# First half of the first key and value projection computed between the two halves of the modulation

## What is computed

```python
mod_lat = silu(c) @ w_mod[l] + b_mod[l]          # [3*1024]; the same for c_ctx
shift, scale, gate = split(mod, 3)
h = rms_norm(x, norm_g) * (1 + scale) + shift    # latent and context rows, each with its own modulation
p = h @ w_in                                     # [512, 11424], split into columns:
qc, kvc, kr, dq, dk, dv, sq, sk, sv, z, gm = split_cols(p)
# kvc and kr: the compressed keys and values (256 columns) and the rotary key (32 columns)
```

## Time and profile before

| | |
|---|---|
| median of three runs | 2431.78 us |
| the profiled execution's own time | 2431.57 us |
| its span, from first to last instruction | 2429.8 us |
| PE busy | 2398.9 us, 99% |
| DVE busy | 1459.4 us, 60% |
| ACT busy | 1192.1 us, 49% |
| DMA in the first of 40 slices (60.7 us) | 7 tenths busy, 258 GB/s |

### The profile page before, as it was taken

One profiled execution on the slowest core, in us unless ns is written; L12 is line 12 of the kernel. 1 busy time (PEld: TensorE's weight loads), 2 busy tenths in 40 slices (PEclk: granted clock), 3 DMA queues, 4 the chain that ended last, 5 costly groups with the idle time before them and its releaser, 6 DMA issues.

```text
span 2429.8 us, 33585 instructions
## 1 busy us (share of the span) xinstructions
PE 2398.9 (99%) x12793; PEld 2013.3 (83%) x12793; DVE 1459.4 (60%) x2470; ACT 1192.1 (49%) x2278; POOL 100.0 (4%) x151
## 2 busy tenths in 40 slices
PE   8999999999999999899999999999999999999999
PEld 6978888788888888888887888888888888888887
DVE  4555564775667435565538676665679844566565
ACT  5553223743247332564337455564566555545643
POOL 1100000510000000000004000000000000000000
PEclk9999999999999999999999999999999999999999
DMA  7403543134430222234531523555555561655653
GB/s 258 109 23 113 165 148 87 45 119 133 147 87 10 91 84 80 80 105 139 144 90 61 178 84 100 198 172 186 178 177 178 190 189 52 208 176 161 201 170 131
DMA packets 165007, 318.80 MB, mean 131 GB/s; under 512 B 10470, under 2 KB 22624, under 8 KB 164336
## 3 DMA queue, kind: packets, MB, share of 16 engines
q1 hardware_dynamic: 161552, 303.67, 40.3%
q0 software_dynamic: 3296, 12.98, 1.9%
HBM read 313.46 MB, written 3.15 MB: 130 GB/s over the span
## 4 chain that ended last, share of the span: by engine, by line
PE 93%; DVE 3%; ACT 2%; issue 1%; DMA 1%; SPq 0%; POOL 0%; DVEq 0%; ACTq 0%
PE bank L895 25%; PE bank L897 24%; PE bank L896 24%; PE bank L937 7%; PE bank L1086 6%; PE bank L1048 1%; PE bank L1059 1%; PE bank L1065 1%; PE bank L1062 1%; PE bank L1213 1%; PE bank L1147 1%; DMA w_raw_more<-in_w_mod_dram 1%; DVE w_low_part L1807 0%; PE bank L1173 0%; PE bank L971 0%
## 5 line engine op out<-in xcount | busy, mean ns | idle before, releaser
L1807 DVE TENSOR_TENSOR w_low_part<-w_raw,w_high_part 128x1024 fp32r<-128x1024 f32 (+3 forms) x544 | 638.3, 1186 | 529.7 <-ACT w_high_part L1289 525.4
L1289 ACT ACTIVATE w_high_part<-w_raw 128x1024 fp32r<-128x1024 f32 (+3 forms) x544 | 553.9, 1031 | 711.0 <-PE bank L897 708.9
L895 PE MATMUL bank<-w_high_part,h_high 128*128 128x512 f32 (+3 forms) x2128 | 816.6, 384 | 3.6 <-DVE h_low L1845 1.7
L897 PE MATMUL bank<-w_high_part,h_low 128*128 128x512 f32 (+3 forms) x2128 | 806.8, 379 | 0.0
L896 PE MATMUL bank<-w_low_part,h_high 128*128 128x512 f32 (+3 forms) x2128 | 805.9, 379 | 0.0
L895 PEld LDWEIGHTS bank<-w_high_part,h_high 128*128 128x128 f32 x2128 | 400.1, 188 | 79.7 <-issue 3.9
L897 PEld LDWEIGHTS bank<-w_high_part,h_low 128*128 128x128 f32 x2128 | 399.9, 188 | 75.1
L896 PEld LDWEIGHTS bank<-w_low_part,h_high 128*128 128x128 f32 x2128 | 400.4, 188 | 71.1 <-issue 0.2
L1620 ACT ACTIVATE stage<-bank,neg_max 128x512 f32<-128x512 f32 (+1 forms) x240 | 147.6, 617 | 112.6 <-DVE neg_max L2290 59.6
L1086 PE MATMUL bank<-v,probs_turned 128*128 128x128 f32 x1280 | 173.3, 275 | 0.0
L937 PEld LDWEIGHTS bank<-ident,stage 128*128 128x128 f32 (+1 forms) x1112 | 127.1, 139 | 52.3 <-issue 35.6
(11 more groups left out here) (318 smaller groups left out, 2550.0 us busy)
## 6 DMA issues: line engine op xcount, KB each, us to landing
w_raw<-in_w_in_dram SPq DMA_DIRECT2D x160, 512.0 KB, 3.6
w_raw<-in_a_w_in_dram SPq DMA_DIRECT2D x96, 512.0 KB, 4.1
w_raw<-in_b_w_in_dram SPq DMA_DIRECT2D x80, 512.0 KB, 4.6
w_raw<-in_w_branch_dram SPq DMA_DIRECT2D x48, 512.0 KB, 4.0
w_raw<-in_w_mod_dram SPq DMA_DIRECT2D x37, 512.0 KB, 4.0
w_raw<-in_a_w_out_dram SPq DMA_DIRECT2D x32, 512.0 KB, 4.2
w_raw<-in_c_w_in_dram SPq DMA_DIRECT2D x32, 512.0 KB, 4.1
w_raw<-in_w_out_dram SPq DMA_DIRECT2D x16, 512.0 KB, 3.9
```

Source lines behind the costliest of these rows:

```text
L895: pe.matmul(o, high, wh, start=(k == 0), stop=False)
L897: mm = pe.matmul(o, low, wh, start=False, stop=(k == u.kt - 1))
L1289: nc.scalar.activation(WH[:, n % PART_SLOTS, 0:kt, 0:width], raw[:, 0:kt, 0:width], ACT.Copy).then_inc(*S.up("w_high", c))
L1807: v.tensor_tensor(WL[:, s, 0:kt, 0:width], raw[:, 0:kt, 0:width], WH[:, s, 0:kt, 0:width].bitcast(F32), ALU.subtract).then_inc(*S.up("w_lo ...
```

## The change

Two of the four chunks of the first `kvc` projection are computed ahead of the last quarter of the work on the modulation. In the new order the list is: mod 0, mod 2, split of h0 and h1, split of h2 and h3, a new step `begin`, the rest of mod 1, mod 3, split of h4 to h7, and `kvc` with its chunks 2 and 3.

- On PE, `begin` is: `kvc` chunk 0 (24 matmuls), rides of the first three chunks of mod 1, `kvc` chunk 1 (24 matmuls). Then come the ride of the fourth chunk of mod 1 and mod 3 as before.
- The transposes h2 and h3 stand right behind `select` of mod 2, in the banks "out" (6 and 7). `select` of mod 1 and of mod 3 also use the banks "out".
- ACT and DVE prepare `kvc` chunk 0 at the head of the split of h0 and h1, chunk 1 behind the split of h3, chunk 2 behind h5, chunk 3 behind h7.
- The transfers go in the new order: mod 0, mod 2, `kvc` chunks 0 and 1, mod 1, mod 3, `kvc` chunks 2 and 3. The landing places follow: mod 1 lands in the places 7, 11, 8 and 12, which mod 2 had, so each of its transfers waits until the ride of mod 2 from that place is done.

```diff
-FIRST_LANDING = (7, 11, 8, 12, 5, 9, 6, 10, 0, 1, 2, 3, 4, 8, 12, 11, 0, 1, 2, 3, 4)
+FIRST_LANDING = (5, 9, 6, 10, 7, 11, 8, 12, 0, 1, 7, 11, 8, 12, 2, 3, 4, 0, 1, 2, 3)
...
+    def place_first(u, count):
+        u.pfirst = len(to_split)
+        u.opened = count
+        for chunk in u.chunks[:count]:
+            u.at.append(len(chunks))
+            to_split.append(len(chunks))
+            chunks.append(chunk)
+        steps.append(("begin", u))
...
             steps.append(("split_h", (0, 1)))
+            steps.append(("split_h", (2, 3)))
+            kvc = Unit("mla_c", ("kvc", l), ALL_TILES, ("h", l), w_in, D, OFF_KV, KVR + ROT, off=QR)
+            place_first(kvc, 2)
             place(modulation_unit(0, 1))
-            steps.append(("split_h", (2, 3)))
             place(modulation_unit(0, 3))
...  PE
+            def begin(u):
+                sums = [other for other in units if other.key == ("mod", 0, 1)][0]
+                chunks_of(u, None, 0, 1)
+                for n in range(3):
+                    ride(sums, n, "out")
+                chunks_of(u, None, 1, 2)
+
             def gemm(u, turned):
                 if u.kind == "mod":
                     j = u.key[2]
-                    for n in range(len(u.chunks)):
+                    for n in range(3 if j == 1 else 0, len(u.chunks)):
                         if (j, n) == (2, 1):
                             select(0, 0, "wide")
                         if (j, n) == (3, 2):
-                            select(0, 1, "wide")
-                        for k in {(2, 2): (0,), (2, 3): (1,), (1, 3): (2,), (3, 0): (3,)}.get((j, n), ()):
+                            select(0, 1, "out")
+                        for k in {(2, 2): (0,), (2, 3): (1,)}.get((j, n), ()):
                             turn(*h_piece(0, k, "turn"))
                         ride(u, n, "out" if j % 2 else "wide")
...
                 elif j > 1:
-                    select(l, j, "wide")
-                    if j == 3:
-                        for k in (6, 7):
-                            turn(*h_piece(0, k, "out"))
+                    select(l, j, "wide" if j == 2 else "out")
+                    for k in (2, 3) if j == 2 else (6, 7):
+                        turn(*h_piece(0, k, "out"))
...  ACT (DVE alike)
-                    if u.key[2] == 3:
-                        prepare(1)
                     take_modulation(u.key)
-                    if u.key[2] == 3:
-                        prepare(2)
...
+            def begin(u):
+                prepare(2)
+
             def split_h(which):
+                if which[0] == 0:
+                    prepare(1)
...
-                    if k > 4:
-                        prepare(k - 3)
+                    if k in (5, 7):
+                        prepare(3 if k == 5 else 4)
```

More of the change, by code:

```diff
@@ L153, in __init__ @@
         self.pfirst = self.plast = None
+        self.opened = 0
 def plan():
@@ L167, in plan @@
     riding = [(sums, m) for sums in (modulation_unit(*lj) for lj in SUMMED) for m in range(D // (P * KT))]
+    def place_first(u, count):
[6 more added lines that the diff above has]
+        steps.append(("begin", u))
     def place(u):
-        u.pfirst = len(to_split)
-        for n, chunk in enumerate(u.chunks):
+        if not u.opened:
+            u.pfirst = len(to_split)
+        for n, chunk in list(enumerate(u.chunks))[u.opened:]:
             u.at.append(len(chunks))
@@ L214, in plan @@
             steps.append(("turn_h", l, 1))
-        gemm("mla_c", ("kvc", l), ALL_TILES, ("h", l), w_in, D, OFF_KV, KVR + ROT, off=QR)
+        if l == 0:
+            place(kvc)
+        else:
+            gemm("mla_c", ("kvc", l), ALL_TILES, ("h", l), w_in, D, OFF_KV, KVR + ROT, off=QR)
         steps.append(("mla_norm", l, "kv", ALL_TILES))
@@ L849, in turn_late @@
                     late.append((n, piece))
+            def begin(u):
[4 more added lines that the diff above has]
+                chunks_of(u, None, 1, 2)
             def gemm(u, turned):
-                open_banks = {}
                 if u.kind == "mod":
                     j = u.key[2]
-                    for n in range(len(u.chunks)):
+                    for n in range(3 if j == 1 else 0, len(u.chunks)):
                         if (j, n) == (2, 1):
@@ L858, in gemm, with chunks_of @@
                         if (j, n) == (3, 2):
-                            select(0, 1, "wide")
-                        for k in {(2, 2): (0,), (2, 3): (1,), (1, 3): (2,), (3, 0): (3,)}.get((j, n), ()):
+                            select(0, 1, "out")
+                        for k in {(2, 2): (0,), (2, 3): (1,)}.get((j, n), ()):
                             turn(*h_piece(0, k, "turn"))
                         ride(u, n, "out" if j % 2 else "wide")
-                    if j == 3:
-                        for k in (4, 5):
-                            turn(*h_piece(0, k, "turn"))
+                    for k in (4, 5) if j == 3 else ():
+                        turn(*h_piece(0, k, "turn"))
                     return
-                for n, (src, k0, kt, col, width) in enumerate(u.chunks):
+                chunks_of(u, turned, u.opened, len(u.chunks))
+                if turned and not turns_inside(u):
+                    turn_qk(turned)
+            opened = {}
+            def chunks_of(u, turned, start, stop):
+                open_banks = opened.setdefault(u.key, {})
+                for n, (src, k0, kt, col, width) in list(enumerate(u.chunks))[start:stop]:
                     while late and late[0][0] <= n:
@@ L903, in gemm @@
                             mm.then_inc(*S.up("w_used", c))
-                if turned and not turns_inside(u):
-                    turn_qk(turned)
             def ride(u, n, pool="out"):
@@ L1246, in store @@
                 pass
-            todo = dict(gemm=gemm, vectors=vectors, condition=condition, modulation=modulation, norm=norm, small=small,
+            todo = dict(gemm=gemm, begin=begin, vectors=vectors, condition=condition, modulation=modulation, norm=norm, small=small,
                         turn_h=turn_h, split_h=split_h, turn_h2=turn_h2, mla_norm=mla_norm, turn_c=turn_c,
@@ L2068, in modulation @@
                 key = ("turn", "mod", l, j)
-                if (l, j) == (0, 3):
-                    prepare(1)
                 dve.wait_ge(*S.filled(key))
@@ L2174, in split_h @@
                                     ALU.subtract).then_inc(*S.up("spare_read", key))
-                    if k > 3:
-                        prepare(max(2, k - 3))
+                    if k in (5, 7):
+                        prepare(3 if k == 5 else 4)
                 spares[0] += len(which)
```

## The result

| | before | changed |
|---|---|---|
| median of 12 runs each | 2431.91 us | 2437.14 us |
| lowest to highest | 2431.21 to 2434.23 | 2435.84 to 2441.99 |
| profiled execution, its span | 2429.8 us | 2435.2 us |
| T, ACT's first h4 | 36.46 | 42.68 |
| start of `qc` | 50.13 | 55.55 |

The changed kernel is slower: ratio 1.0023, 95% interval 1.0015 to 1.0031, 5.2 us. The last row says where: everything behind the start of `qc` takes the same time, so the whole difference is made in the first 56 us.

A forecast was written before the change was run, and what follows sets the result against it. Before, transfers bound the modulation until 34 us; changed, PE's own queue would end it and the split stand uncovered. T 43.7 plus 12.2 puts `qc` at 55.9 against 50.13, +5.8 us: 2437.4 us, range 2434.3 to 2440.3.

The forecast's parts named there:

- T: ACT's first h4, after the modulation: forecast to move from 36.46 to 43.7 us.
- the forecast's own range: Total time of the changed kernel, central case: 2436.6 to 2438.8 us around 2437.4, given 55%.
- S: Start of kvc chunk 1 on PE: forecast 34.5 us, bounds 33.4 and 35.9.
- First fall of the clock: PE at kvc chunk 0: clock low from 28.0 to 31.4 us, 0.26 us a matmul, chunk ending at 32.85.
- T to qc: From ACT's first h4 to the start of `qc`: 12.2 us with a clock fall at chunk 2, bounds 12.0 and 13.7.
- The transfers don't set it: End of the modulation: last transfer lands near 34.8 us, but PE asks for it only at 40.7.
- Preparation of chunk 0 and the banks cost nothing: ACT and DVE prepare chunk 0 within existing waits, charged nothing; copies from banks 6 and 7 are over in time.
- Order on PE: PE's queue: matmuls stay in program order, so no ride can overtake kvc chunk 0 or 1.
- (a): Rival: inserted 6.3 us hide in PE's transfer waits, `qc` at 50.0, kernel not slower at 2431.5 us; 12%.
- (b): Rival: the clock doesn't fall, or falls once, giving 2436.0 to 2436.8 us; 22%.
- (c): Rival: the clock stays low through all of chunk 0 and chunk 2, giving 2439 to 2440.3 us; 11%.

The follow-up runs named there:

- e4: The kernel before, with SP issuing the first kvc transfer only after the ride of the first chunk of mod 3: 2431.90 us, ratio to before 0.9996 to 1.0014.
- e11: The kernel before plus the same single unused matmuls behind most rides as e10, as a control: 2431.51 us.
- e3: The changed kernel plus unused matmuls in two PE waits, 7 ahead of kvc chunk 0 and 10 ahead of chunk 2: 2438.94 us.
- e6: As e3, with two more unused matmuls behind each ride of mod 0 and mod 2, to hold the clock: 2436.31 us.
- e7: As e2, only kvc chunk 0 early, with the unused matmuls of e6 but none ahead of chunk 2: 2432.35 us.
- e1: The changed kernel with no kvc chunk early on PE, all four behind h7; transfers and preparation as changed: 2432.61 us.
- e2: The changed kernel with only kvc chunk 0 ahead of the rides on PE, chunk 1 behind h7 again: 2433.83 us.
- e9: The kernel before without its warm-up matmuls: 2432.03 us, ratio to before 0.9992 to 1.0010.
- e5: PE's order as in the kernel before, only transfers and preparation of kvc chunks 0 and 1 early as changed: 2432.26 us.
- e10: As e5, with one unused matmul behind most rides: 2432.36 us.
- e8: The changed kernel without the 26 warm-up matmuls of PE at the start: 2440.08 us.
- e12: Against the kernel before, only kvc chunk 0 sent ahead of mod 1, its four row tiles computed one by one between rides: 2435.44 us.

## Why the prediction was right

The time was 2437.14 for 2437.4 forecast, inside the forecast's own range, and slower.

- **T.** Forecast 43.7, measured 42.68. The step from S to T was 9.2 and is 9.11 (33.57 to 42.68). S was 0.9 early, since chunk 0 began at 27.15 instead of 28.0. That goes back to the last ride of mod 2, at 21.46 instead of 22.40 in the trace of before, which seems to have been a late one: e4, with the same transfers up to there, has it at 21.44, but e11 at 22.76.
- **First fall of the clock.** Forecast low from chunk 0's start to 31.4, measured from 28.0 to 31.4. The price was right, the path in part luck: chunk 0's first 0.8 us ran at 1.00, and the clock came back 4.3 us after its start, where I had 3.4. A matmul at 1.2 GHz took 0.24 us, where I had 0.26. Chunk 0 took 5.0 us, the forecast 4.85.
- **T to qc.** Forecast 12.2, measured 12.87. The chain of the split was right to a tenth: chunk 2 at T + 4.2 (46.88), the low part of chunk 3 at T + 8.0. Too small was the time for which the clock stays down: I took 3.4 us from the start of chunk 2, but it was low from 45.0 to 51.9, 5.0 us of chunk 2, which took 5.5 us instead of 4.85. My three distances were also read a little long: by the slices of the earlier trace rows the clock came back 3.0 and 3.5 us after PE's restart, where I wrote 3.3 and 3.7, and fell 2.9 us after its stop, where I wrote 3.1. In the changed kernel it came back 4.3 and 5.0 us after, so no single distance from the trace of before would have served. With the clock held it is 12.07 (e3, e6, e7), as the lower bound of 12.0 had it. The errors of -1.0 at T and +0.7 behind it nearly cancel, which is luck; the sum came out better than its terms.
- **The transfers don't set it.** Right: the queues are empty from 36 to 39 us, the last ride starts at 39.8, and e1 with all transfers as changed takes 2432.6.
- **Preparation of chunk 0 and the banks cost nothing.** Right: ACT's first h0 stands 0.20 behind `h_scale`, as before, and DVE's first low part of h 2.18 behind that, where it was 2.19. That e1's rides would wait for h2's bank was not seen ahead of the experiment; in the changed kernel chunk 0 hides it.
- **Order on PE.** Right: e1 and e2 show the time following the place of the chunks in PE's queue.
- **Rivals.** (a), that the work is hidden, holds for chunk 0 alone with the clock held (e7, 2432.35, of which some 1.5 are fillers), not for both. The times of (b) and (c) are near the two ends of the changed kernel's runs (2435.84 and 2441.99), but no trace shows the clock in those. e6, with no fall at all, lies below the (b) bound once its fillers are taken off.

The split between order and clock, 3.3 and 2.1 us, was only worked out ahead (4.5 with no fall at all, 5.8 with both); the 4.5 was 1.2 too high, in large part for the same late ride.

## What to carry to other kernels

An idle stretch of an in-order engine can be filled only up to the point at which the next transfer lands; what is put in beyond that pushes everything behind it. Count the engine's work between the two points, not its idle share. Work that covers another engine's chain isn't free to move: look at what the chain looks like without it, and count the clock that TensorE loses in the hole. And a stretch bound by transfers hides a low clock as long as TensorE keeps up with them at that clock: of 2.8 us, e9 kept 0.6 at T. Once it doesn't, as in the profiled execution of e5, the same stretch loses some 7 us (`qc` at 56.85 against 50.07 in e10). Bound by TensorE there is no such slack: e8 kept all 2.3.

## What the runs showed of the hardware

The clock can stay low although PE is shown as busy. In the windows of e5 it was low from 18.2 to 45.5 us, with rides, `select` and transposes nearly back to back, and came back 2.5 us after the first matmul of the projection, at 43.0:

```profile
20.00:25.00 5.00, 4.51 (x30) 2.06 (x27) 0.00 (x0) 0.86 (x2) 0.00 (x0) 0.50 1.06 388
35.00:40.00 5.00, 5.00 (x33) 3.57 (x32) 1.06 (x3) 0.44 (x2) 1.49 (x2) 0.50 0.61 189
45.00:50.00 5.00, 5.00 (x38) 5.00 (x37) 3.36 (x6) 2.99 (x7) 0.00 (x0) 0.95 0.30 80
```

Yet sixteen transposes alone had brought it back in the second layer, at 1002.3 us. What makes the difference was not tried by itself. The Trainium skill (TensorE: Matmul & The Clock Gate, "Part 4: PE-mode transpose") says that the full clock doesn't set in for transposes; e5 would fit that, don't. Not expected either: the state of the clock in the first 45 us differs from execution to execution of one kernel. In e1 to e5 and e12 the runs of one kernel lie 4.4 to 7.4 us apart, and the slowest run of each has the lowest mean clock of its kernel; with fillers behind the rides and in the waits (e6, e7) they lie 1.2 and 0.6 apart.
